# One Strassen unit in the output product, with its four left sums on GpSimd

## The reference

```python
proj = rmsnorm(h, norm_mix_g[i]) @ w_in[i]
# y_a: gated MLP in chunks (width 1024), y_b: state-space mixer with a norm per group (width 1024)
h = h + jnp.concatenate([y_a, y_b], axis=-1) @ w_out[i]        # (512 x 2048) @ (2048 x 1024)
hid = relu(rmsnorm(h, norm_mlp_g[i]) @ w_ff1[i]);  h = h + (hid * hid) @ w_ff2[i]
gate = sigmoid(rmsnorm(h, ple_norm_g[i]) @ w_ple_gate[i]);  h = h + gate * (p[i] @ w_ple_proj[i])
```

## Time and profile before

| | |
|---|---|
| median of 3 runs | 725.94 us (725.80 to 725.96) |
| the profiled execution | 725.95 us, its span 724.2 us |
| PE busy | 715.8 us, 3904 matmuls |
| DVE busy | 534.5 us |
| ACT busy | 418.1 us |
| POOL busy | 134.9 us |
| mean granted clock of TensorE | 0.997 of full |

### The profile page before, as it was taken

One profiled execution on the slowest core, in us unless ns is written; L12 is line 12 of the kernel. 1 busy time (PEld: TensorE's weight loads), 2 busy tenths in 40 slices (PEclk: granted clock), 3 DMA queues, 4 the chain that ended last, 5 costly groups with the idle time before them and its releaser, 6 DMA issues.

```text
span 724.2 us, 9904 instructions
## 1 busy us (share of the span) xinstructions
PE 715.8 (99%) x3904; PEld 616.1 (85%) x3904; DVE 534.5 (74%) x572; ACT 418.1 (58%) x533; POOL 134.9 (19%) x111
## 2 busy tenths in 40 slices
PE   9999999999999999999999999999999999999996
PEld 7788877888888888888899889988999889988884
DVE  6798784567666465655889975999579957898874
ACT  7754556645665833414776834683358535673885
POOL 1040001765464000001110212121111221020000
PEclk9999999999999999999999999999999999999998
DMA  9932123332431163128867897899887997887311
GB/s 332 314 117 87 59 88 117 117 117 87 164 128 58 63 215 131 56 91 232 206 143 218 184 295 176 218 197 290 168 209 203 250 236 168 214 175 266 112 60 58
DMA packets 53447, 119.83 MB, mean 165 GB/s; under 512 B 5372, under 2 KB 5528, under 8 KB 53400
## 3 DMA queue, kind: packets, MB, share of 16 engines
q1 hardware_dynamic: 40888, 85.60, 34.7%
q0 software_dynamic: 11136, 29.36, 22.3%
q10 hardware_dynamic: 1376, 4.23, 1.7%
HBM read 98.18 MB, written 4.23 MB: 141 GB/s over the span
## 4 chain that ended last, share of the span: by engine, by line
PE 99%; ACT 0%; issue 0%; DVE 0%; ACTq 0%
PE acc L1730 28%; PE acc L1732 28%; PE acc L1731 28%; PE side L1830 3%; PE side L1730 2%; PE side L1731 2%; PE side L1732 2%; PE side L1921 2%; PE side L1888 1%; PE side L1928 1%; PE side L1916 1%; PE acc L1847 1%; PE side L1869 0%; PE side L1868 0%; PE side L1908 0%; PE acc L1739 0%
## 5 line engine op out<-in xcount | busy, mean ns | idle before, releaser
L804 ACT ACTIVATE ring_hi<-quarter 128x1024 fp32r<-128x1024 f32 x112 | 113.6, 1051 | 100.8 <-PE acc L1732 49.5
L1488 DVE TENSOR_TENSOR ring_lo<-quarter,ring_hi 128x1024 fp32r<-128x1024 f32 x112 | 132.8, 1219 | 36.3 <-ACT ring_hi L804 36.1
L1730 PE MATMUL acc<-w_hi,a_hi 128*128 128x512 f32 x252 | 102.7, 407 | 0.0
L1732 PE MATMUL acc<-w_hi,a_lo 128*128 128x512 f32 x252 | 98.4, 391 | 0.0
L1731 PE MATMUL acc<-w_lo,a_hi 128*128 128x512 f32 x252 | 98.2, 390 | 0.0
L662 POOL DMA_DIRECT2D quarter<-in_w_ff x24 | 29.2, 1220 | 235.4 <-DMA quarter<-in_w_ff 235.2
L1731 PE MATMUL acc<-xS_lo,ring_hi 128*128 128x256 f32 x256 | 72.4, 283 | 0.0
L1731 PEld LDWEIGHTS acc<-w_lo,a_hi 128*128 128x128 f32 x252 | 47.4, 188 | 10.9 <-issue 1.7
L1730 PEld LDWEIGHTS acc<-w_hi,a_hi 128*128 128x128 f32 x252 | 47.4, 188 | 10.9 <-issue 1.7
L1732 PEld LDWEIGHTS acc<-w_hi,a_lo 128*128 128x128 f32 x252 | 47.3, 188 | 10.2
L1732 PE MATMUL acc<-xA_hi,ring_lo 128*128 128x256 f32 x192 | 54.3, 283 | 0.0
(11 more groups left out here) (303 smaller groups left out, 1836.3 us busy)
## 6 DMA issues: line engine op xcount, KB each, us to landing
quarter<-in_w_ff SPq DMA_DIRECT2D x72, 512.0 KB, 5.6
w_raw<-in_w_in SPq DMA_DIRECT2D x32, 512.0 KB, 3.6
quarter<-quarter POOLq DMA_DIRECT2D x32, 512.0 KB, 7.9
quarter<-in_w_ff POOLq DMA_DIRECT2D x24, 512.0 KB, 7.8
w_raw<-in_w_out SPq DMA_DIRECT2D x16, 512.0 KB, 3.2
h<-in_x SPq DMA_DIRECT2D x8, 512.0 KB, 5.8
seg<-cs_dram ACTq DMA_DIRECT2D x8, 512.0 KB, 3.8
w_raw<-in_w_ple_gate SPq DMA_DIRECT2D x8, 512.0 KB, 5.1
```

The costliest lines, as they stand in the source:

```text
L804: act.activation(ring[n % 3][0][at], quarter[i][at], ACT.Copy).then_inc(form_hi, 1)
L1488: dve.tensor_tensor(lo[at], src, hi[at].bitcast(F32), ALU.subtract).then_inc(form_lo, 1)
L1730: pe.matmul(dst, st[0], mv[0], start=start, stop=False)
L1732: return pe.matmul(dst, st[1], mv[0], start=False, stop=stop)
```

## The change

The y_b half of the output product, 512 x 1024 times 1024 x 1024, becomes one Strassen unit. Its left operand is cut into quarters A11 to A22 (256 positions by 512), its weights into B11 to B22 (512 x 512), its result into the quarters h11 to h22 of h. There are seven products (`yb_product`), each of 24 matmuls of 512 columns: B11 with A11, T2 with S2, T3 with S3, T1 with S1, B21 with A12, B22 with S4, T4 with A22, in this order. T1 to T4 are sums of weights, made by eight adding DMAs out of POOL's queue, in place in `w_raw`. S1 to S4 are differences of left quarters, which POOL makes by four `tensor_tensor` of 128 x 1024 in place in `y`. The products T3 and T1 go to banks of `side`, the others to `acc`.

Since sums mix tiles, y_b is scaled ahead of its transposes (`scale_y`, ACT), and no longer in the add to h; the transposes are evacuated by ACT alone into `y` in 128 x 128 pieces with the norm's gain as scale (`raw_evac`), which until now was the scale of the weight split. hi and lo of the quarters A11, A12 and A22 and of the four sums are then made out of `y`. The y_b transposes now stand behind t = 38 to 41. h21 and h12 are brought into another basis before the products are added, and back after (`yb_add`, 13 DVE adds in place of 8). Norm, transposes and x_evac of the tiles come after the products, around PLE. Of the loads, w_ple and the first quarters of w_ff1 are placed anew; some semaphores are shared or renamed. The core of it, cut, with the start of each line shifted left:

```diff
+YB_FORMS = ("B11", "T1", "T2", "T3", "B21", "B22", "T4")
+YB_PRODUCTS = ("B11", "T2", "T3", "T1", "B21", "B22", "T4")
+YB_SLOT = {"B11": 0, "T1": 1, "T2": 2, "T3": 3, "B21": 0, "B22": 2, "T4": 3}
+YB_SUMS = ("S1", "S3", "S2", "S4")
+YB_SPLITS = ("S2", "S3", "S1", "S4")
+YB_ADDS = ("h21 basis", "h12 basis", "B11 right", "B11", "T2", "h12 back", "T3", "h21 back", "T1 right", "T1", "B21",
+           "B22", "T4")
+YB_LOADS = {"B11": (0, 1), "B12": (1, 1), "B21": (1, 2), "B22": (1, 3)}
+YB_MADE = {"T3": (1, 1), "T1": (0, 2), "T2": (0, 3), "T4": (0, 4)}
...
-load_rows(OUT + 2, w_out, 8)
+def load_yb(q, k, c, last=None):
+    for p in range(2):
+        if last is None:
+            sp.wait_ge(lo_ready, 4 * (OUT + 1) + 2 * q + p + 1)
+        else:
+            sp.wait_ge(yw_lo, 2 * YB_FORMS.index(last) + p + 1)
+        sp.dma_start(w_raw[:, 2 * q + p], w_out[:, k + 2 * p:k + 2 * p + 2, c:c + 512]
+                     ).then_inc(w_landed[2 * q + p], 16)
+load_yb(0, 8, 0)
+load_yb(1, 8, 512)
 sp.wait_ge(yb_mul, 8)
 sp.dma_start(tmp[:, 0:2, :], p_dram).then_inc(p_landed, 16)
-load_rows(OUT + 3, w_out, 12)
...
+load_yb(1, 12, 0, "T3")
+load_yb(1, 12, 512, "B21")
...
+def yb_sum(q, k, c, p, last=None):
+    if last is None:
+        pool.wait_ge(w_landed[2 * q + p], 16 * (OUT + 2))
+    else:
+        pool.wait_ge(yw_lo, 2 * YB_FORMS.index(last) + p + 1)
+        if last == "B11":
+            pool.wait_ge(ysum_landed[p], 16)
+    pool.dma_start(w_raw[:, 2 * q + p], w_out[:, k + 2 * p:k + 2 * p + 2, c:c + 512], accum_op=ALU.add
+                   ).then_inc(ysum_landed[p], 16)
+for p in range(2):
+    yb_sum(1, 12, 512, p)
+for p in range(2):
+    yb_sum(0, 8, 512, p, "B11")
+for p in range(2):
+    yb_sum(0, 12, 512, p, "T1")
+def yb_a_sum(name):
+    left, right = {"S1": ("A21", "A22"), "S3": ("A21", "A11"), "S2": ("A11", "S1"), "S4": ("A12", "S2")}[name]
+    if name == "S1":
+        for q in range(2):
+            for s in range(NS):
+                wait_free(pool, ("yt", 2 + q, s))
+        pool.wait_ge(yr_ready, 6 * NS)
+        pool.wait_ge(yb_lo, 6)
+    else:
+        pool.wait_ge(ys_sum, YB_SUMS.index(name))
+    pool.tensor_tensor(yb_part(y, name), yb_part(y, left), yb_part(y, right), ALU.subtract).then_inc(ys_sum, 1)
+for name in YB_SUMS:
+    yb_a_sum(name)
+for p in range(2):
+    yb_sum(0, 12, 0, p, "T2")
...
+            act.wait_ge(*added("B22" if s < 2 else "T4"))
...
+def raw_evac(s):
+    for q in range(2):
+        name = ("yt", 2 + q, s)
+        bank = wait_full(act, name)
+        for k in range(4):
+            at = slice(k * P, k * P + P)
+            ins = act.activation(y[:, s, 512 * q + k * P:512 * q + k * P + P], bank[:, at], ACT.Copy,
+                                 scale=cols[:, 84 + 4 * q + k:85 + 4 * q + k])
+            if k < 3:
+                ins.then_inc(yr_ready, 1)
+            else:
+                freed(ins, name)
...
+def split_sum(name):
+    act.wait_ge(ys_sum, len(YB_SUMS))
+    act.activation(yb_sum_hi(name), yb_part(y, name).rearrange("p i (k t) -> p i k t", t=P), ACT.Copy
+                   ).then_inc(ys_hi, 1)
+def split_yb(n):
+    for p in range(2):
+        piece, landed, count = yb_raw(n, p)
+        act.wait_ge(landed, count)
+        if n < 4:
+            act.wait_ge(acc_full, 4 * (OUT + 1) if n < 2 else 4 * (OUT + 2))
+        else:
+            act.wait_ge(yb_full, n - 3)
+        act.activation(yb_weights(w_hi, n)[:, 2 * p:2 * p + 2], w_raw[:, piece], ACT.Copy
+                       ).then_inc(yw_hi, 1)
...
+raw_evac(0)
+split_yb(0)
+raw_evac(1)
+raw_evac(2)
+raw_evac(3)
+split_yb(1)
+for name in YB_SPLITS:
+    split_sum(name)
+for k in range(2):
+    act.wait_ge(p_landed, 16)
+    act.activation(p_hi[:, k, :], tmp[:, k, :], ACT.Copy).then_inc(pt_hi, 1)
+for n in range(2, 7):
+    split_yb(n)
+for p in (2, 3, 0, 1):
+    split_hi(PLE, p)
+sums(1, 0)
+sums(1, 1)
+x_evac(0)
+x_evac(1)
+for p in range(2):
+    split_form(0, p)
+sums(1, 2)
+sums(1, 3)
...
+def yb_add(what):
+    dst, src, op = {
+        "h21 basis": (h21, h22, ALU.add), "h12 basis": (h12, h22, ALU.subtract),
+        "B11 right": (h22, acc[:, 0:2, :], ALU.subtract), "B11": (h11, acc[:, 0:2, :], ALU.add),
+        "T2": (h22, acc[:, 2:4, :], ALU.add), "h12 back": (h12, h22, ALU.add),
+        "T3": (h22, side[:, 0:2, :], ALU.add), "h21 back": (h21, h22, ALU.subtract),
+        "T1 right": (h22, side[:, 2:4, :], ALU.add), "T1": (h12, side[:, 2:4, :], ALU.add),
+        "B21": (h11, acc[:, 0:2, :], ALU.add), "B22": (h12, acc[:, 2:4, :], ALU.add),
+        "T4": (h21, acc[:, 0:2, :], ALU.add)}[what]
...
+raw_split(3)
+split_yb(1)
+add_group(OUT + 1, 2)
+split_sum("S2")
+add_group(OUT + 1, 3)
+yb_add("h21 basis")
+split_yb(2)
+yb_add("h12 basis")
+split_yb(3)
+split_sum("S3")
+yb_add("B11 right")
+yb_add("B11")
+split_sum("S1")
+split_yb(4)
+yb_add("T2")
+yb_add("h12 back")
+split_sum("S4")
+split_yb(5)
+yb_add("T3")
+yb_add("h21 back")
+for k in range(2):
+    dve.wait_ge(pt_hi, k + 1)
+    dve.tensor_tensor(p_lo[:, k, :], tmp[:, k, :], p_hi[:, k, :].bitcast(F32), ALU.subtract
+                      ).then_inc(pt_lo, 1)
+split_yb(6)
+yb_add("T1 right")
+yb_add("T1")
+yb_add("B21")
+for p in (2, 3, 0, 1):
+    split_lo(PLE, p)
+yb_add("B22")
+normed(0)
+normed(1)
+x_evac(0)
+x_evac(1)
+yb_add("T4")
+for p in range(2):
+    split_form(0, p)
+normed(2)
+normed(3)
...
+def yb_product(form, name, bank):
+    at, n = yb_operand(name), YB_FORMS.index(form)
+    if name[0] == "A":
+        pe.wait_ge(yb_lo, 6 if name == "A22" else 4)
+    else:
+        pe.wait_ge(ys_lo, YB_SPLITS.index(name) + 1)
+    for i in range(2):
+        for k in range(4):
+            if i == 0 and k % 2 == 0:
+                pe.wait_ge(yw_lo, 2 * n + k // 2 + 1)
+            ins = product(bank[:, i, :], at(i, k), [yb_weights(t, n)[:, k, :] for t in (w_hi, w_lo)],
+                          k == 0, k == 3)
+    ins.then_inc(yb_full, 1)
...
+pe.wait_ge(*emptied(OUT + 1, 2))
+yb_product("B11", "A11", acc[:, 0:2])
+pe.wait_ge(*emptied(OUT + 1, 3))
+yb_product("T2", "S2", acc[:, 2:4])
+for q in range(2):
+    wait_free(pe, ("yt", 2 + q, 2))
+yb_product("T3", "S3", side[:, 0:2])
+for q in range(2):
+    wait_free(pe, ("yt", 2 + q, 3))
+yb_product("T1", "S1", side[:, 2:4])
+pe.wait_ge(*added("B11"))
+yb_product("B21", "A12", acc[:, 0:2])
+pe.wait_ge(*added("T2"))
+yb_product("B22", "S4", acc[:, 2:4])
+pe.wait_ge(*added("B21"))
+yb_product("T4", "A22", acc[:, 0:2])
+pe.wait_ge(*added("T1"))
+turn_norm(1, 0)
+turn_norm(1, 1)
 pe.wait_ge(pt_lo, 2)
 for s in range(4):
+    if s < 2:
+        pe.wait_ge(*added(("T4", "B22")[s]))
     group_pair(PLE, s, (p_hi, p_lo), 0, nk=2)
-    if s == 1:
-        turn_norm(1, 3)
+    if s in (1, 2):
+        turn_norm(1, 1 + s)
```

261 lines of the change are left out of this document (153 added, 108 removed).

## The result

| | before | after |
|---|---|---|
| median | 725.91 us (725.80 to 725.96, 4 runs) | 747.11 us (745.48 to 747.43, 4 runs) |
| the profiled execution | 725.95 us, span 724.2 us | 747.38 us, span 745.3 us |
| TensorE matmuls | 3904 | 3880 |
| mean granted clock | 0.997 | 0.981 |

The ratio of the times is 1.0288, with a 95% interval of 1.027 to 1.0306. The change costs 21 us; the forecast was 737, with a range of 730 to 743. The direction was right, the size was outside the range.

The account below looks back on a forecast made before the run. TensorE was taken to bound the kernel, busy 715.8 of 724.2 us. 725.95 - 5.45 + 5.6 + 0.2 + 6.9 = 733.2, plus 4.0 for two clock falls, gave 737.2, rounded to 737; range 730 to 743.

Parts of the forecast that it names:

- (1): Up to B11's end: no TensorE wait, B11 done at 302.8; the 24 matmuls removed save 5.45 us.
- (2): The four left sums on GpSimd: start at 293.4, take 7.9 us in all, end at 301.3.
- Rival (b): GpSimd's sums are stretched to 2.4 or 2.94 us each: 739 to 741 with two falls; chance 0.18.
- (3): Ahead of T2: its weight split queues behind the sums, ACT last; TensorE waits 5.6 us, until 308.5.
- (4): Products after T2: T3 waits 0.2 us, the rest are in time; thinnest margin 0.9 us, B21's add before T4.
- (5): Last add to PLE: waits of 1.0 and 0.6 us at the transposes, 5.3 ahead of PLE; 6.9 together.
- (6): Feed-forward part: bound by TensorE, operands ready in time, gives nothing back; no time added.
- (7): TensorE's clock falls twice, in the gaps of (3) and (5), at 2.0 us each: 4.0 us.
- Rival (c): TensorE meets no gap because the output stage's side work lies earlier: 720.5 us; chance 0.03.

Follow-up runs that it names:

- the experiment on ACT alone: The changed kernel with T2's weights split ahead of the four sum splits in ACT's queue only: 744.82 us, ratio 1.0251.
- reordered version: The changed kernel with the left sums on VectorE and splits, basis changes, w_ple loads, T4's add and norms reordered by need: 728.56 us, ratio 1.0038.
- the filled version: The changed kernel with 34 matmuls of 512 columns that nobody reads between the B11 and T2 products: 744.79 us, ratio 1.0256.
- loads moved: Reordered version with T4's adding DMAs held until B21's weights land, w_ff1 quarters B12 and B11 loaded first, some splits and x_evac moved: 730.53 us.
- four additions on GpSimd: The loads moved kernel with the basis changes and their reversals on GpSimd instead of VectorE, and some splits, an add and a load moved: 732.88 us.
- reordered, sums on GpSimd: Reordered version with the four left sums back on GpSimd and the basis changes ahead of S2's split on DVE: 736.80 us, ratio 1.0143.

## Why the prediction was wrong, point by point

**(1), 24 matmuls for 5.45 us: right.** 3880 matmuls, and the pitch of 0.227 in the T2 product where the clock is full. B11's last matmul starts at 302.83, so the product ends at 303.06 (forecast 302.8).

**(2), the start of the sums: right; their duration: a term too small.** 293.79 for 293.4, but 2.37 to 2.96 each instead of 1.94: 10.35 us instead of 7.9, so that they end 2.8 us late. I had L618 of the earlier trace rows at 2.40 and 3.27 in front of me and took L606 because its form reads nearest. A row of the timeline doesn't tell whether the two inputs are two regions. The experiment with one operand twice shows that this makes 0.50 of it. Rival (b) had the longer sums with their price, at 0.18. At 2.4 a sum, which is what the trace shows for three of the four, it gave 739. The prediction's other estimate, 2.4 us for a sum (by the Trainium skill, "GPSIMD Engine Reference", section "Elementwise — side-by-side cycle accounting", 1.96 times DVE's), agrees with the trace: 2.394 to 1.22 is 1.96.

**(3), ACT's queue ends last and T2 waits: right in place and order, 8.24 for 5.6.** T2 starts at 311.46 for 308.5, and the late end of the sums makes 2.8 of these 3.0. That ACT and DVE are nearly equally late in it (308.5 and 307.3 in the forecast) is shown by the experiment on ACT alone, which won 1.3.

**(4), "this is the thinnest margin, 0.9 us": right that it is thin, wrong that it holds.** The T4 product waits 1.31 for the addition of B21. The forecast took DVE's load as the sum of the steps it listed; the trace has DVE behind with B21's and B22's weights, which landed late (ACT waits 9.74 us for B21's up to 322.64 and 4.01 for B22's up to 328.88), and then without a break from 333.15 to 342.7. The fastest reordered version shows the same pair, a load that comes late and a full queue of DVE behind it; none of the runs takes away the one and keeps the other, so their shares stay open.

**(5), from the last addition to PLE: the second wait right, the first missed.** My chain left out w_ple: I took it as landed, with the 2.5 us of the earlier trace rows, though ACT's and DVE's splits of it stand ahead of the addition of B22. In the kernel after its issue stands behind 2 MB of quarters whose issue itself waits for TensorE's products. Moving it ahead took the wait from 4.15 to 0.87. This is the step that failed outright: the forecast had 1.0 us of wait here and the trace has 4.15, with 2.0 us of slow transposes behind it. I had gone through four queues and not through SP's; the text on the change said that w_ple and the quarters are placed anew. PLE's wait was 3.46 for 5.3 because the transposes before it were slow and covered 2 us of it.

**(6), the feed-forward part needs nothing: wrong by 0.9 to 2.1 us here.** And it was the reason that later gains were not kept. In all reordered versions TensorE waits there (0.47 and 1.81 us in the fastest); I take it that the left operands, made later than in the kernel before, are the reason, but the rows give no engine for these waits.

**(7), two falls of the clock: right; 2.0 each: too small.** The fall in T2 costs 2.67, the second one 2.40 in PLE and 2.04 in the transposes: 7.1 instead of 4.0. The second lasted from about 351 through the transposes and PLE's wait, which is why it was paid in two places. My own rows had given 2.7 as the upper end and I took less.

Together: the terms were short by 2.6 (3), 1.3 (4), 3.1 (5, first wait), 3.1 (7) and 2.1 (6), and long by 1.8 (5, PLE), 0.6 (5, second tile) and 0.2 (4, T3). That is 9.6 of the 10.2 us by which the profiled 747.38 exceeds the sum of 737.2; 0.3 lie outside the span and 0.3 before the feed-forward part. No single term is large, and no rival had them all: the forecast had the direction and the first place, it had the wait ahead of T2 and the price of a fall too small, and it had the waits ahead of T4, of the transposes and in the feed-forward part at nothing or nearly so. The range fell short because it took these terms as unlikely to go wrong together, while each was read at its nearest or cheapest row.

**Rival (c), faster at 720.5,** wanted no wait at all. The reordered version is the nearest to it and stays at 728.56, slower than before by 0.26 to 0.51%. None of the versions beats the kernel before, so none is put forward.

## What to carry to other kernels

In a kernel whose busiest engine has no gaps, a cut in its work is worth what the other queues can follow. So go through every queue that the change touches, the one that issues loads included, and look for what stands ahead of each step before you price the step itself. A gap of TensorE costs its length and, often, a slow restart behind it, and a repair of one gap tends to come back at the next engine: look at which queue is second in each place before you count a gain.

## What the runs showed of the hardware

- **GpSimd and VectorE slow each other when both read two regions of SBUF.** DVE's split of 1.22 us takes 3.41 and 3.44 beside a GpSimd addition, and the GpSimd addition 3.3 instead of 2.4. The rows fit with each waiting until the other's instruction has ended: both slow splits end 1.09 us behind a GpSimd addition. A DVE instruction with an input in PSUM isn't slowed (1.28, beside a sum of 2.40). The Trainium skill ("GPSIMD Engine Reference", section "Key points") states a contention with DVE instructions that have two SBUF inputs; the trace agrees, and the size, 2.2 us more for an instruction of 1.22, is from these rows.
- **A GpSimd subtraction of 128x1024 lasts 1.895 us with one region as both inputs and 2.394 with two.** That is with VectorE idle beside it.
- **The length of a wait alone doesn't say whether the clock falls.** Behind each of TensorE's waits of 2.88 us and more that these rows show, the clock was at 0.50 in the wait or within 1.1 us of its end. It also fell behind one of 2.06 (reordered), one of 2.12 (loads moved) and, 1.3 us later, one of 1.74 (four additions on GpSimd). It stayed at 1.00 behind waits of 1.31 (the change), 2.05 (one operand), 2.09 (reordered, sums on GpSimd) and 2.40 (T2 split first). What else decides is not shown.
- **A fall cost 1.5 to 2.8 us in the 24 matmuls behind it,** of which the first run at half the pitch. The least is the T4 product of the filled version (6.97 instead of 5.44), the most PLE's first 24 in the same version (8.25). Matmuls that nobody reads kept the clock up: 34 of them left T2's start where it was (311.49 for 311.46). When they outlast the wait they cost time: 20 of them moved the transposes by 1.84 us.
- **The landing of a load depends on what stands ahead of it.** The 256 KB pieces of w_ple took 6.8 to 9.4 us behind 2 MB in the same queue (the change, the filled version, T4 added early), and 2.5 to 3.5 without (before, w_ple first, reordered, loads moved).
